# Late modulation columns turned by TensorE and added by VectorE, ahead of a level's attention transposes

## The reference

```python
def hybrid_layer(x, c, ...):
    mod = jax.nn.silu(c) @ ada_w + ada_b          # (1, 1024) @ (1024, 6144)
    sh_m, sc_m, gt_m, sh_f, sc_f, gt_f = jnp.split(mod[:, None, :], 6, axis=-1)
    h = rms_norm(x, norm_mix) * (1 + sc_m) + sh_m
    ...
    x = x + gt_m * (jnp.concatenate([o_a, o_b, o_c], axis=-1) @ w_out)
    h = rms_norm(x, norm_ffn) * (1 + sc_f) + sh_f
    gate, up = jnp.split(h @ w_gate_up, 2, axis=-1)
    return x + gt_f * ((jax.nn.silu(gate) * up) @ w_down)
```

## Time and profile before

| | |
|---|---|
| median of 3 runs | 1533.38 us (1533.18, 1533.38, 1537.52) |
| span of the profiled execution | 1530.9 us |
| PE busy | 1476.5 us (96%), 11522 matmul instructions |
| PE weight loads busy | 1365.5 us (89%) |
| DVE busy | 1015.0 us (66%) |
| ACT busy | 791.7 us (52%) |
| POOL busy | 301.7 us (20%) |
| DMA | 287.73 MB, mean 188 GB/s |

### The profile page before, as it was taken

How to read it: one execution, slowest core, us unless ns; L and a number is a source line. 1 busy time by engine, 2 the same in 40 slices (tenths; PEclk the granted TensorE clock), 3 DMA queues, 4 the chain that set the end, 5 groups by cost and what they waited for, 6 DMA issues and landing times.

```text
span 1530.9 us, 27684 instructions
## 1 busy us (share of the span) xinstructions
PE 1476.5 (96%) x11522; PEld 1365.5 (89%) x11522; DVE 1015.0 (66%) x1386; ACT 791.7 (52%) x1332; POOL 301.7 (20%) x190
## 2 busy tenths in 40 slices
PE   7999999999999999999999997999999999999997
PEld 3997889999889978899998897889998999999986
DVE  1785456877767854577546777758786656587754
ACT  3774355443357543654435555456554556566542
POOL 0002211999930032149100001100000001000000
PEclk9999999999999999999999999999999999999999
DMA  9455575675644365255435643244535544345442
GB/s 385 185 200 226 192 254 204 241 270 203 246 186 181 125 256 193 103 220 220 177 141 206 228 166 111 110 165 183 202 131 189 203 165 147 128 166 185 166 167 88
DMA packets 31931, 287.73 MB, mean 188 GB/s; under 512 B 3079, under 2 KB 11559, under 8 KB 12488
## 3 DMA queue, kind: packets, MB, share of 16 engines
q1 hardware_dynamic: 27400, 267.15, 46.9%
q0 software_dynamic: 2304, 16.78, 3.0%
q10 hardware_dynamic: 2112, 2.15, 0.5%
HBM read 284.97 MB, written 7.39 MB: 191 GB/s over the span
## 4 chain that ended last, share of the span: by engine, by line
PE 80%; DVE 9%; ACT 7%; issue 2%; DMA 1%; POOL 1%; POOLq 0%; SPq 0%; DVEq 0%; ACTq 0%
PE bank L675 16%; PE bank L676 16%; PE bank L677 16%; PE bank L1147 10%; PE bank L1148 5%; PE bank L1092 2%; ACT w_hi L1527 2%; DVE w_lo L2082 2%; PE bank L988 1%; PE bank L1006 1%; PE bank L795 1%; PE bank L836 1%; PE bank L809 1%; PE bank L1004 1%; PE bank L824 1%
## 5 line engine op out<-in xcount | busy, mean ns | idle before, releaser
L675 PE MATMUL bank<-hi_T,w_hi 128*128 128x256 f32 (+1 forms) x2056 | 588.4, 286 | 9.6 <-DVE mix_lo L2109 4.0
L2082 DVE TENSOR_TENSOR w_lo<-ring,w_hi 128x2048 fp32r<-128x2048 f32 (+3 forms) x215 | 483.2, 2257 | 160.6 <-ACT w_hi L1527 158.4
L677 PE MATMUL bank<-hi_T,w_lo 128*128 128x256 f32 (+1 forms) x2056 | 582.5, 283 | 0.0
L676 PE MATMUL bank<-h_lo,w_hi 128*128 128x256 f32 (+1 forms) x1928 | 545.7, 283 | 0.0
L1527 ACT ACTIVATE w_hi<-ring 128x2048 fp32r<-128x2048 f32 (+3 forms) x215 | 372.1, 1732 | 244.6 <-PE bank L677 109.3
L675 PEld LDWEIGHTS bank<-hi_T,w_hi 128*128 128x128 f32 (+1 forms) x2056 | 394.8, 192 | 15.8 <-DVE mix_lo L2109 4.5
L677 PEld LDWEIGHTS bank<-hi_T,w_lo 128*128 128x128 f32 (+1 forms) x2056 | 394.9, 192 | 0.0
L676 PEld LDWEIGHTS bank<-h_lo,w_hi 128*128 128x128 f32 (+1 forms) x1928 | 369.8, 192 | 0.6 <-issue 0.2
L1147 PE MATMUL bank<-act_both,w_hi 128*128 128x512 f32 x672 | 238.2, 398 | 1.2 <-DVE w_lo L2082 1.2
L1148 PE MATMUL bank<-act_both,w_lo 128*128 128x256 f32 x672 | 188.4, 280 | 0.0
L1147 PEld LDWEIGHTS bank<-act_both,w_hi 128*128 128x128 f32 x672 | 126.2, 188 | 30.6 <-DVE w_lo L2082 1.6
(11 more groups left out here) (290 smaller groups left out, 2005.6 us busy)
## 6 DMA issues: line engine op xcount, KB each, us to landing
ring<-w_gu SPq DMA_DIRECT2D x22, 2048.0 KB, 7.8
ring<-w_dn SPq DMA_DIRECT2D x32, 1408.0 KB, 6.1
ring<-w_up SPq DMA_DIRECT2D x22, 2048.0 KB, 7.7
ring<-ada SPq DMA_DIRECT2D x16, 2048.0 KB, 8.6
ring<-w_mix SPq DMA_DIRECT2D x11, 2048.0 KB, 8.3
arena<-ada POOLq DMA_DIRECT2D x16, 1024.0 KB, 6.9
ring<-even_in SPq DMA_DIRECT2D x8, 2048.0 KB, 7.8
ring<-odd_in SPq DMA_DIRECT2D x6, 2048.0 KB, 7.7
```

Of the source, the lines that this page charges most:

```text
L675: nc.tensor.matmul(out, wh, xh, start=start, stop=False)
L676: nc.tensor.matmul(out, wh, xl, start=False, stop=False)
L677: return nc.tensor.matmul(out, wl, xh, start=False, stop=stop)
L2082: V.tensor_tensor(w_lo[:, n % SLOTS, at], ring[:, n % SLOTS, at], w_hi[:, u % AHEAD, 0:size].bitcast(F32), ALU.subtract).then_inc(w_lo_rea ...
```

## The change

For chunks 4 to 23 the products with a column of ones are replaced by four transposes per chunk (`turn`) into a bank of their own, 512 columns, and one sum by DVE (`turned_sum`) that writes the four columns of `mod` directly: over four elements for a dotted chunk, over 128 for a late one. Bank 7 serves dotted chunks and even late ones, bank 6 or 3 the odd late ones. Two semaphores are new, `mod_turned` (PE to DVE, ACT and POOL) and `mod_added` (DVE to PE). In a mixing level `turn` stands where `modulations` stood, the attention transposes follow at once, and the first half of the dots stands behind them, waiting for `mod_added` since it writes bank 7; ACT's order is changed accordingly. In dn0 the wait of PE for `mod_read` is replaced by one for `gemm_freed` ahead of each turn.

```diff
@@ -155,6 +155,12 @@
     def halves_before(m):
 
         return 6 * (m // ADA_L) + m % ADA_L - ADA_FIRST
+
+    def turn_bank(m):
+
+        if ada_at[m] is not None or m % 2 == 0:
+            return 7
+        return 3 if ADA_L <= m < ADA_L + ADA_FIRST else 6
 
     def ada_bank(m):
 
@@ -367,6 +373,8 @@
         mod_ready = sem("mod_ready")
         late_in = [sem(f"late_in{half}") for half in range(2)]
         mod_read = sem("mod_read")
+        mod_turned = sem("mod_turned")
+        mod_added = sem("mod_added")
         sq_ready = sem("sq_ready")
         sq_added = sem("sq_added")
         ssq_ready = sem("ssq_ready")
@@ -787,6 +795,8 @@
                 if half == 0:
                     chunk_in(ada_at[m])
                     pe.wait_ge(acc_ready, m)
+                    if m > ADA_FIRST:
+                        pe.wait_ge(mod_added, m - ADA_FIRST)
                 else:
                     pe.wait_ge(half_copied, halves_before(m) + 1)
                 w = ring[:, ada_at[m] % SLOTS, :].rearrange("p (k n) -> p k n", k=KT)
@@ -802,13 +812,19 @@
                     pe.wait_ge(acc_ready, m + 1)
                     for t in range(4):
                         at = MOD_COL + 4 * m + t
-                        if ada_at[m] is not None:
-                            sums_m, ones = acc[:, m % 2, :], const("pick")[:, 0:1]
-                        else:
-                            sums_m, ones = late_sums[:, m % 2, :], const("ones")[:, 0:1]
-                        last = nc.tensor.matmul(bank[:, 7, at:at + 1], sums_m[:, t * P:t * P + P], ones,
+                        last = nc.tensor.matmul(bank[:, 7, at:at + 1], acc[:, m % 2, t * P:t * P + P], const("pick")[:, 0:1],
                                                 start=True, stop=True)
                     last.then_inc(mod_ready, 1)
+
+            def turn(m):
+
+                pe.wait_ge(acc_ready, m + 1)
+                if m > ADA_FIRST:
+                    pe.wait_ge(mod_added, m - ADA_FIRST - (0 if ada_at[m] is not None else m % 2))
+                sums_m = acc[:, m % 2, :] if ada_at[m] is not None else late_sums[:, m % 2, :]
+                for t in range(4):
+                    last = nc.tensor.transpose(bank[:, turn_bank(m), t * P:t * P + P], sums_m[:, t * P:t * P + P], ident)
+                last.then_inc(mod_turned, 1)
 
             def scores(u):
                 U = units[u]
@@ -989,11 +1005,10 @@
                                                     X[:, ch, :] if lv else ident, start=True, stop=True)
                         last.then_inc(t1_ready, 1)
                     if lv:
-                        modulations(m + lv - 1, m + lv)
-                    if lv < 6:
-                        half_dots(m + lv, 0)
+                        turn(m + lv - 1)
                     if lv < LEVELS - 1:
                         transposes(u0 + lv)
+                        half_dots(m + lv, 0)
                     for half in range(2 if lv else 0):
                         pe.wait_ge(t1_copied, l * 2 * (LEVELS - 1) + 2 * (lv - 1) + half + 1)
                         if half:
@@ -1124,9 +1139,9 @@
                         one(j, i * (2 * SLOTS) + u0 + 2 * j + 1, i * (4 * SLOTS) + t0 + 4 * j - 3)
                 if m_next:
                     chunks(5, 6)
-                    modulations(m_next - 1, m_next)
+                    turn(m_next - 1)
                     chunks(6, 9)
-                    modulations(m_next, m_next + 1)
+                    turn(m_next)
                     chunks(9, 11)
                 else:
                     chunks(8, 11)
@@ -1155,9 +1170,9 @@
 
                     if name == "dn0" and j in NEXT_ADA:
                         m = ADA_L + NEXT_ADA.index(j)
-                        if m == ADA_L:
-                            pe.wait_ge(mod_read, 2)
-                        modulations(m, m + NEXT_ADA.count(j))
+                        pe.wait_ge(gemm_freed, ph["t0"])
+                        for late_m in range(m, m + NEXT_ADA.count(j)):
+                            turn(late_m)
 
                 pe.wait_ge(hidden_ready, done - 5)
                 part_sum(0, 0)
@@ -1552,8 +1567,10 @@
             def ada_half(m, half):
 
                 act.wait_ge(rows_ready, 2 * on_pe.index(m) + half + 1)
-                if half == 0:
+                if half == 0 and m < ADA_FIRST + 2:
                     act.wait_ge(mod_ready, m - 1)
+                elif half == 0:
+                    act.wait_ge(mod_turned, m - 1 - ADA_FIRST)
                 nc.scalar.activation(acc[:, m % 2, half * S:half * S + S], bank[:, 7, 0:S], ACT.Copy)\
                     .then_inc(acc_ready if half else half_copied, 1)
 
@@ -1700,8 +1717,8 @@
                         exps(u0 + lv + 1)
                         copy_pt(u0 + lv)
                         break
+                    copy_pt(u0 + lv)
                     ada_half(m + lv, 0)
-                    copy_pt(u0 + lv)
                     ada_half(m + lv, 1)
                     exps(u0 + lv + 1)
 
@@ -2307,6 +2324,7 @@
             def mixing(l):
 
                 u0 = stages[f"hybrid{l}"][0]
+                m = ADA_L * l + ADA_FIRST
 
                 logits(u0)
                 for b in range(4):
@@ -2322,6 +2340,8 @@
                 logits(u0 + 1)
                 for lv in range(LEVELS):
                     there = 0 if lv % 2 else 2
+                    if lv:
+                        turned_sum(m + lv - 1)
                     for half in range(2):
                         hs = slice(4 * half, 4 * half + 4)
                         if lv == 0:
@@ -2438,9 +2458,12 @@
                     low(ph["u0"] + AHEAD)
                     low(ph["u0"] + 1 + AHEAD)
                 for k in range(KT):
+                    if name == "dn0" and k in NEXT_ADA:
+                        m = ADA_L + NEXT_ADA.index(k)
+                        for late_m in range(m, m + NEXT_ADA.count(k)):
+                            turned_sum(late_m)
                     if name == "dn0" and k == KT - 1:
 
-                        dve.wait_ge(mod_ready, ADA_L + ADA_FIRST)
                         modulation(1, 0, ADA_FIRST)
                         norm_gain(1, 0).then_inc(mod_read, 2)
                         dve.wait_ge(mod_read, 4)
@@ -2491,11 +2514,26 @@
                 if r1 == 8:
                     ch(V.tensor_scalar(selm[:, qt, 0:w], work[:, 0, 0:w], -2e38, NEG, ALU.is_gt, ALU.mult))
 
+            def turned_sum(m):
+
+                dve.wait_ge(mod_turned, m - ADA_FIRST + 1)
+                at = 4 * (m % ADA_L)
+                rows = bank[:, turn_bank(m), :].rearrange("p (t g n) -> p t g n", t=4, g=4)
+                if ada_at[m] is not None:
+                    V.tensor_reduce(out=mod[:, m // ADA_L, at:at + 4], in_=rows[:, :, :, 0], op=ALU.add, axis=AX.X)\
+                        .then_inc(mod_added, 1)
+                else:
+                    V.tensor_reduce(out=mod[:, m // ADA_L, at:at + 4], in_=rows, op=ALU.add, axis=AX.XY)\
+                        .then_inc(mod_added, 1)
+
             def modulation(l, m0, m1, read=None):
 
-                at = MOD_COL + 4 * ADA_L * l
-                ins = V.tensor_tensor(mod[:, l, 4 * m0:4 * m1], bank[:, 7, at + 4 * m0:at + 4 * m1],
-                                      vec(l, "ada_b")[:, 4 * m0:4 * m1], ALU.add)
+                out, sums_m = mod[:, l, 4 * m0:4 * m1], mod[:, l, 4 * m0:4 * m1]
+                if l == m0 == 0:
+                    sums_m = bank[:, 7, MOD_COL:MOD_COL + 4 * m1]
+                else:
+                    dve.wait_ge(mod_added, ADA_L * l + m1 - ADA_FIRST)
+                ins = V.tensor_tensor(out, sums_m, vec(l, "ada_b")[:, 4 * m0:4 * m1], ALU.add)
                 if read:
                     ins.then_inc(read, 1)
                     dve.wait_ge(read, 2 + 3 * l)
@@ -2527,7 +2565,6 @@
                 input_columns(l)
                 mixing(l)
 
-                dve.wait_ge(mod_ready, m + 6)
                 modulation(l, ADA_FIRST, ADA_L - 2)
                 ch(norm_gain(l, 1))
                 dve.wait_ge(w_lo_ready, phases[f"out{l}"]["u0"] + AHEAD)
@@ -2567,10 +2604,12 @@
                 with dve.Fori(0, 2) as i:
                     for j in range(1, 1 + SLOTS):
                         gate_chunk(j, i)
+                turned_sum(m + 6)
                 for j in range(1 + 2 * SLOTS, 11):
                     gate_chunk(j)
-
-                dve.wait_ge(mod_ready, m + 8)
+                    if j == 8:
+                        turned_sum(m + 7)
+
                 modulation(l, ADA_L - 2, ADA_L, mod_read)
                 if l == L1 - 1:
                     dve.wait_ge(vec2_in, 16)
@@ -2817,7 +2856,7 @@
                                             along(c_silu[:, k:k + 1], CH), ALU.mult))
                 ch.wait()
                 if half == 0:
-                    pool.wait_ge(mod_ready, m - 1)
+                    pool.wait_ge(mod_turned, m - 1 - ADA_FIRST)
```

## The result

The changed kernel takes 1543.47 us (median; 1541.21 to 1547.98), the kernel before 1533.97 beside it: a ratio of 1.0067, interval 1.0053 to 1.0081. Slower was the likelier side of the forecast, but 1543.5 lies above the range, which ended at 1541.8. The profiled execution of the changed kernel took 1541.21 us, with a span of 1539.4; the span of before was 1530.9, so **8.5 us** have to be found, where the prediction had 4.9.

A forecast was written before the change was run, and what follows sets the result against it. TensorE (PE), 80% of the span's chain, was taken to bound the kernel. Span 1530.9 + 6.9 (mixing) - 2.0 (gu and dn) = 1535.8, with 2.5 from span to median 1538.3 us; range 1534.8 to 1541.8.

The forecast's parts named there:

- "plus 1.00" for the moved dots: Mixing levels: the first half of the dots, moved behind the attention transposes, puts 1.00 us ahead of T1's products.
- The clock's falls: In the new PE gaps of level 1 the clock halves, costing up to 1.7 us a fall; chance 0.20.
- gates: Mixing levels: the moments when attention transposes may start, set by POOL's probabilities or DVE's logits; nothing moves them.
- Levels: +3.45 a layer: Mixing, per layer: 0.05 in level 0, 1.00 in levels 1 and 5, 0.40 in levels 2 to 4, 0.2 in level 6.
- T: Mixing levels: the end of issue of the level's first products (L988), where L809 starts.
- Small sums: ready before the dots, 0.2 in level 6: Mixing: DVE's sums end under the four transposes, so dots do not wait; in level 6 the sum adds 0.2 us.
- 0.45 for each turned late chunk: gu and dn: four transposes replace 0.90 us of products in dense PE streams, saving 0.45 us a chunk.
- gu and dn: -2.0, since POOL binds at chunk 15: gu and dn: 1.15 us saved in layer 0, where PE waits for POOL's last sum, and 0.9 in layer 1.
- Late sums hidden: gu and dn: DVE's eight late sums, 0.69 us each and 5.5 in all, fall in DVE's waits.
- "Other new waits: nothing": Waits for mod_added at a turn and for mod_turned on ACT and POOL look at the level before, costing nothing.
- The rule of the Trainium skill on transposes: Transposes do not count as PE activity in the same way, so the exchange would add clock falls; chance left at 0.20.
- Outside the span +2.5: Whole kernel: the median of the runs shown lies 2.5 us above the span, added to the predicted span.

The follow-up runs named there:

- Run 1: Kernel before with only the order changed: attention transposes ahead of the first half of the dots, nothing turned; 1544.9 us, ratio 1.0073.
- run 2: Changed kernel with the order of before in mixing (first half of the dots ahead of the attention transposes), turning kept; 1536.96 us, ratio 1.0021.
- run 4: Kernel before with only the eight late chunks turned, their sums written to PSUM; 1532.48 us, ratio 0.9995.
- runs 3 to 5: Kernel before with only late chunks turned, sums in SBUF (1533.37 us) or PSUM (1532.48 us); changed kernel with late sums in PSUM (1543.21 us).
- run 11: Changed kernel with the four transposes of the turn in level 1 of each layer made four times over; 1540.47 us, ratio 1.0054.

## Why the prediction was wrong

**The direction and the main mechanism were right; the size was not.** The forecast was 1538.3 and 1543.5 was measured, 5.2 above: 3.6 in the span of the profiled execution and 1.6 between that execution and the median. Two steps failed: the "plus 1.00" for the moved dots, which left out their passage behind the transposes, and the place where POOL binds in dn0. The clock's falls, a rival, came on top. The saved 0.54 us a level is lost in gates that did not move, the dots that used to fill the wait stand behind it, and mixing pays more than gu and dn give. Run 1 shows that in the new order it is the order alone that pays. Point by point:

- *Levels: +3.45 a layer.* Mis-sized: 4.39, 1.9 us in both layers. The gates held, L852 starting at T + 2.68 in level 1 and T + 2.03 in level 5 as before. The term that failed is the "plus 1.00" for the moved dots. The dots cost 1.00 and, behind transposes, 0.17 to 0.21 us of a gap that L809 did not have in front of them, 0.01. The misses of levels 0 to 5 are 0.11 to 0.24 each, less 0.16 too much for level 6. The order transposes, dots had no example in the rows of mixing, and I bounded the wait for the sum but not the passage.
- *Small sums: ready before the dots, 0.2 in level 6.* The first part right: 0.17 us each, and no dot waits. In level 6 the sum runs 208.01 to 208.17 and the update starts at 208.09; the cost was 0.04.
- *0.45 for each turned late chunk.* Right: 0.45 to 0.58 in the changed kernel.
- *gu and dn: -2.0, since POOL binds at chunk 15.* The sum of the profiled execution was -1.6 without the clock, nearly the forecast, for another reason. POOL does take back the savings ahead of it, but not at chunk 15, where PE did not wait in the changed kernel: it does so in column 1 of dn0, by holding DVE's split. The forecast wait at chunk 15 is there in run 2, 4.83 us, where POOL gave way to the split instead. Which of the two comes hangs on very little: the split started 0.48 us ahead of POOL's row in the changed kernel and was held, 0.50 ahead in run 2 and was not. The wait stood in the trace of before, 1.56 us for w_lo at 398.11, and I read over it. I looked for POOL where PE uses its product, not where it holds an engine that PE needs. So the gains of chunks 10 to 13 were lost (0.90 + 0.90 against 2.13) and those of 14 and 15 kept.
- *Late sums hidden.* Right: 1.28 us for two (0.69 each was forecast). In run 4 the second x update behind them starts at 390.15, 2.89 ahead of its 393.04 before, as PE is 2.93 ahead there: the sums stand where DVE had 2.83 us of idle time.
- *"Other new waits: nothing", and the add of `ada_b` not costed at all.* The add went from 0.15 to 4.50 us, which I had missed, but it cost nothing, as the next split would have waited instead (runs 3 to 5).
- *The clock, a rival at 0.20.* It came: 1.6 in level 1, as priced, and 1.6 in dn0, which I had not priced, the only wait that I had there being one of 1.5 us. The one at 219.6 went, -1.45. Net +1.8 of the miss. This part is chance in both directions, as falls come and go between executions.
- *The rule of the Trainium skill on transposes.* No run speaks for it: the clock stayed full in run 11, where transposes filled the gap. In the changed kernel it fell where PE also stood still for longer, so that fall doesn't speak for the rule.
- *Outside the span +2.5.* The time outside the span is 1.8 in the profiled execution, and 1.7 to 1.8 in the others. The rest of the 2.5 was that the profiled execution of before is faster than the median, and that differs from kernel to kernel: the changed one was profiled in the fastest of its four executions, and the median lies 2.3 above it. So 4.1 stood where 2.5 was added.
- *The range.* Its low end, "POOL free and the low end of the mixing bound", is 1530.9 + 5.5 - 3.6 + 2.5 = 1535.3 by the prediction's own terms, not 1534.8. It plays no part in the miss.

The miss of the span is 1539.4 - 1535.8 = 3.6: 1.8 for the levels, 0.4 for gu and dn, 1.8 for the clock, less 0.3 at the start (3.7 by these rounded terms). Mixing without the clock, +8.7, lay inside its own bound of +9, and the falls were a rival with a price; the range's upper end held either on top of the centre, but not both at once.

**What stays open.** What the 0.17 to 0.21 us between transposes and dots is made of; that both it and the 0.41 behind the dots are booked as "issue" is all the trace says. What decides whether DVE's split or POOL's weighing is held. Both happen in every trace: of POOL's 64 weighings in the kernel before, some beside a split take 2.1 to 3.1 us instead of 1.03 (the four from 418.01 take 6.80), while the row at 392.53 takes its 4.03 and DVE waits. In column 1 of dn0 a split that started 0.49 us ahead of the row (run 11) was held and one 0.50 ahead (run 2) was not, but recorded starts that close carry no rule. And why the wait for w_lo at 866 us goes with the turned late chunks.
